# A two-block transformer step in float32 on one core: the order of long and short product rows, four more wide phases, loads and ScalarE copies moved, and the norms' squares added by VectorE in place of Pool

## The reference

```
h = rmsnorm(x, ln1)
hq, hk, hv, hr, ha, hatt, hgate = split(h @ w_in)
o = gated_linear_attention(hq, hk, hv, log_sigmoid(ha @ w_a2 + b_a) / 16)   # 4 heads, chunks of 64
y_gla = (norm(o) * gla_gn * silu(hr)) @ w_o_gla
y_att = dilated_attention(hatt, rel_bias) @ w_o_attn                       # 3 groups, 4 heads
x = x + (sigmoid(g_gla) * y_gla + sigmoid(g_att) * y_att) @ w_out
x = x + relu(rmsnorm(x, ln2) @ w_mlp1) ** 2 @ w_mlp2                        # 4096 wide
x = x + sigmoid(rmsnorm(x, ln3) @ w_pg) * (p @ w_pp)
x = rmsnorm(x, ln_f)
for i in (0, 1):                                                            # second block
    x = x + 0.5 * (silu(n(x) @ ffn1_w1) * (n(x) @ ffn1_w3)) @ ffn1_w2       # 2816 wide
    x = x + (conv_module(n(x)) if i == 0 else mla(n(x), positions))
    x = x + 0.5 * (silu(n(x) @ ffn2_w1) * (n(x) @ ffn2_w3)) @ ffn2_w2
return rmsnorm(x, final_norm)
```

## Time and profile before

| | us |
|---|---|
| median of 3 runs | 1534.92 (1533.19 to 1535.77) |
| the profiled execution | 1532.38 |
| its span | 1530.6 |
| PE busy | 1497.5 |
| DVE busy | 1140.8 |
| ACT busy | 740.9 |
| Pool busy | 99.1 |

### The profile page before, as it was taken

The page is one execution under the profiler, slowest core; times in us unless marked ns, Lnnn a source line. Parts: engine busy times, 40 slices in busy tenths (PEclk is TensorE's granted clock), DMA queues, the critical chain, the costliest instruction groups (busy, mean ns, idle before and its releaser), DMA issues.

```text
span 1530.6 us, 25551 instructions
## 1 busy us (share of the span) xinstructions
PE 1497.5 (98%) x9946; PEld 1336.3 (87%) x9946; DVE 1140.8 (75%) x1466; ACT 740.9 (48%) x996; POOL 99.1 (6%) x144
## 2 busy tenths in 40 slices
PE   8999999999999999999998999999999999999997
PEld 6879899998888988888986988898888997888887
DVE  6767766788866678788876877678776687887754
ACT  5535445534434375554544545345544444455443
POOL 1000000002000121000221100010000010100000
PEclk9999999999999999999999999999999999999999
DMA  7636665456655556656632666567665654466553
GB/s 218 186 96 179 182 177 151 141 184 186 191 191 182 163 176 189 191 155 187 211 117 71 183 191 190 155 193 207 191 185 162 200 135 145 125 180 190 162 170 110
DMA packets 268921, 260.15 MB, mean 170 GB/s; under 512 B 15703, under 2 KB 267173, under 8 KB 268827
## 3 DMA queue, kind: packets, MB, share of 16 engines
q1 hardware_dynamic: 267120, 256.41, 56.3%
q0 software_dynamic: 1072, 1.98, 0.5%
q10 hardware_dynamic: 634, 0.44, 0.1%
HBM read 257.73 MB, written 1.07 MB: 169 GB/s over the span
## 4 chain that ended last, share of the span: by engine, by line
PE 60%; DVE 3%; ACT 1%; issue 1%; POOL 0%; ACTq 0%; DVEq 0%
PE ps L598 28%; PE ps L601 14%; PE ps L605 13%; PE misc L807 2%; PE misc L758 1%; DVE rstd L1239 0%; DVE wsplit L1197 0%; PE misc L639 0%; DVE parts L1215 0%; PE misc L635 0%; DVE plain L1267 0%; PE ps L782 0%; PE misc L761 0%; ACT sq L977 0%; DVE x L1376 0%
## 5 line engine op out<-in xcount | busy, mean ns | idle before, releaser
L1197 DVE TENSOR_TENSOR wsplit<-raw,wsplit 128x1024 fp32r<-128x1024 f32 (+2 forms) x532 | 592.1, 1142 | 106.2 <-ACT wsplit L937 94.8
L937 ACT CAST wsplit<-raw 128x1024 fp32r<-128x1024 f32 (+2 forms) x532 | 494.9, 969 | 179.9 <-DMA raw<-in_ffn_w_dram 89.2
L598 PE MATMUL ps<-xa,wsplit 128*128 128x512 f32 x1504 | 528.2, 397 | 0.0
L601 PE MATMUL ps<-xa,wsplit 128*128 128x256 f32 x1504 | 419.9, 279 | 0.0
L598 PEld LDWEIGHTS ps<-xa,wsplit 128*128 128x128 f32 x1504 | 282.5, 188 | 68.9 <-DVE val L1255 1.4
L598 PE MATMUL ps<-parts,wsplit 128*128 128x512 f32 x924 | 325.3, 397 | 0.2 <-DVEq L1250 0.2
L601 PEld LDWEIGHTS ps<-xa,wsplit 128*128 128x128 f32 x1504 | 283.5, 188 | 0.1
L601 PE MATMUL ps<-parts,wsplit 128*128 128x256 f32 x924 | 259.6, 281 | 0.0
L605 PE MATMUL ps<-parts,wsplit 128*128 128x256 f32 x1740 | 215.2, 286 | 9.7 <-DVE parts L1234 5.5
L605 PEld LDWEIGHTS ps<-parts,wsplit 128*128 128x128 f32 x1740 | 212.1, 194 | 11.1 <-issue 5.9
L965 ACT COPY lohalf<-ps 128x512 f32<-128x512 f32 x140 | 82.0, 586 | 277.0 <-PE ps L601 277.0
(11 more groups left out here) (254 smaller groups left out, 1119.0 us busy)
## 6 DMA issues: line engine op xcount, KB each, us to landing
raw<-in_ffn_w_dram SPq DMA_DIRECT2D x176, 512.0 KB, 3.8
raw<-in_w_in_dram SPq DMA_DIRECT2D x76, 512.0 KB, 3.7
raw<-in_ffn_w_dram SPq DMA_DIRECT2D x96, 384.0 KB, 3.2
raw<-in_w_mlp_dram SPq DMA_DIRECT2D x64, 512.0 KB, 3.7
raw<-in_conv_w_pw_dram SPq DMA_DIRECT2D x24, 512.0 KB, 4.2
raw<-in_ffn_w_dram SPq DMA_DIRECT2D x32, 256.0 KB, 3.1
raw<-in_w_o_gla_dram SPq DMA_DIRECT2D x8, 512.0 KB, 3.4
raw<-in_w_out_dram SPq DMA_DIRECT2D x8, 512.0 KB, 3.4
```

Source lines behind the costliest of these rows:

```text
L598: mm(o, still, both.rearrange("p h t -> p (h t)"), start=st, stop=False, skip_group_check=True)
L601: last = mm(o[:, T:2 * T], still, moves, start=False, stop=en, skip_group_check=True)
L937: nc.scalar.copy(wsplit[:, slot, 0:kn, 0, 0:p.width], raw[:, slot, 0:kn, 1, 0:p.width]).then_inc(hi_done, 1)
L1197: TT(wsplit[:, slot, 0:kn, 1, 0:p.width], raw[:, slot, 0:kn, 1, 0:p.width], wsplit[:, slot, 0:kn, 0, 0:p.width].bitcast(F32), ALU.subtract ...
```

## The change

It does seven things.

1. In wide groups that aren't the first of their phase, PE takes all long rows of a block and then all short ones in even blocks, and all short ones and then all long ones in odd blocks. With layout F the long rows of an even block wait for the high parts only.
2. hr, w_out, pw2 and w_o join the wide phases.
3. DVE adds the squares (`add_squares`), two chunks side by side, in the groups that make x; Pool keeps only the sum of the norm "conv".
4. ACT issues one load (ln1) at the start; the other eleven loads of gains and the six of the setup go behind the norm step of ha. PE turns the gains and computes the relative bias after the second group of gla_q. The first split of x takes two steps.
5. ACT copies the turned probabilities after the first cast of the group instead of after the second.
6. p is loaded by Pool before the convolution's taps, into other memory, turned by PE after mlp2's first group, copied by DVE there.
7. The norm step of ckv moves behind the evacuation of uq_rope's second group.

```diff
-WIDE = (["gla_q", "gla_k", "gla_v", "mlp1", "mlp2"] + [f"att_{w}{g}" for w in "qkv" for g in range(3)]
+WIDE = (["gla_q", "gla_k", "gla_v", "hr", "w_out", "mlp1", "mlp2", "pw2", "w_o"] + [f"att_{w}{g}" for w in "qkv" for g in range(3)]
...
+                    F = p.layout == "F"
...
+                    def high(kk, c, end):
+                        mov, w, wh, _, mh, _ = operands(kk, c)
+                        still, both = (wh, mov) if F else (mh, w)
+                        return mm(ps[:, bank, c, :], still, both.rearrange("p h t -> p (h t)"),
+                                  start=p.k0[j] + kk == 0, stop=end, skip_group_check=True)
+
+                    def low(kk, c, end):
+                        _, _, wh, wl, mh, ml = operands(kk, c)
+                        still, moves = (wl, mh) if F else (ml, wh)
+                        return mm(ps[:, bank, c, T:2 * T], still, moves, start=False, stop=end, skip_group_check=True)
+
+                    places = [(kk, c) for kk in range(kn) for c in range(p.width // P)]
+                    ends = j == len(p.kns) - 1
+                    if p.halves(g) and not first and j % 2 == 0:
+                        if F:
+                            pe.wait_ge(hi_done, lin(s + 1, RING if i is not None else 0, i))
+                        else:
+                            pe.wait_ge(lo_done, lin(s + 1, RING if i is not None else 0, i))
+                        for kk, c in places:
+                            high(kk, c, False)
+                        if F:
+                            pe.wait_ge(lo_done, lin(s + 1, RING if i is not None else 0, i))
+                        for kk, c in places:
+                            last = low(kk, c, ends and kk == kn - 1)
+                    elif p.halves(g) and not first:
+                        pe.wait_ge(lo_done, lin(s + 1, RING if i is not None else 0, i))
+                        for kk, c in places:
+                            low(kk, c, False)
+                        for kk, c in places:
+                            last = high(kk, c, ends and kk == kn - 1)
+                    else:
+                        pe.wait_ge(lo_done, lin(s + 1, RING if i is not None else 0, i))
+                        for kk, c in places:
+                            k = p.k0[j] + kk
+                            if first and c == 0:
+                                pe.wait_ge(ready, p.ready + k + 1)
+                                high(kk, c, False)
+                                last = low(kk, c, en)
+                                continue
...
-                        if p.name == "ha":
-                            pe.wait_ge(s_rows, 16 * (len(GAINS) - 1))
-                            transpose_to(ps[:, 0, 1, 0:GAIN_N], gain_rows, GAIN_N).then_inc(s_pe, 1)
-                        elif g == 0 and p.name in norm_at:
+                        if g == 0 and p.name in norm_at and p.name != "ha":
...
-                        if p.name == "gla_q" and g == 0:
-                            relative_bias()
+                        if p.name == "gla_q" and g == 1:
+                            pe.wait_ge(s_rows, 16 * (len(GAINS) - 1))
+                            transpose_to(gains_turned, gain_rows, GAIN_N).then_inc(s_pe, 1)
+                            relative_bias()
...
-                        if p.name == "w_pg0":
+                        if p.name == "mlp2" and g == 0:
...
-                                                        plain[:, 40 + t, k * P:(k + 1) * P])
+                                                        unit(64 + t)[:, k * P:(k + 1) * P])
```

ACT, at the start and in the loop over the phases:

```diff
-                act.dma_start(gain_rows[at:at + n, :], v.rearrange("(c p) -> c p", p=P)
-                              ).then_inc(s_ln1 if at == 0 else s_rows, 16)
-                at += n
+            act.dma_start(gain_rows[0:NC, :], a["ln1"].rearrange("a (c p) -> (a c) p", p=P)).then_inc(s_ln1, 16)
...
-                if c == 3:
-                    act.dma_start(wa2[0:GLA_RANK, :], a["w_a2"][0]).then_inc(s_setup, 16)
-                    act.dma_start(wa2[GLA_RANK:GLA_RANK + 1, :], a["b_a"]).then_inc(s_setup, 16)
...
+            def small_inputs():
+
+                at = 0
+                for name, n in GAINS:
+                    v = a[name]
+                    v = v if len(v.shape) == 1 else v.rearrange("a n -> (a n)")
+                    if at:
+                        act.dma_start(gain_rows[at:at + n, :], v.rearrange("(c p) -> c p", p=P)).then_inc(s_rows, 16)
+                    at += n
+                act.dma_start(wa2[0:GLA_RANK, :], a["w_a2"][0]).then_inc(s_setup, 16)
+                act.dma_start(wa2[GLA_RANK:GLA_RANK + 1, :], a["b_a"]).then_inc(s_setup, 16)
...
+                act.dma_start(posi, a["positions_2"][0].partition_broadcast(P)).then_inc(s_setup, 16)
...
+                            if j == 0 and ((p.name == "gates" and g % 2 == 0 and g) or p.name == "y_gla0"):
+                                attend(f"att{g // 2 - 1 if g else 3}", ATT_G, "pT")
                         if g == 0 and p.name in norm_at:
                             norm_step(norm_at[p.name])
+                            if p.name == "ha":
+                                small_inputs()
...
-                        if (p.name == "gates" and g % 2 == 0 and g) or p.name == "y_gla0":
-                            attend(f"att{g // 2 - 1 if g else 3}", ATT_G, "pT")
```

DVE, where the sums of squares are called, the function, and the other moved steps:

```diff
+                    if g:
+                        add_squares("cq" if g < 2 else "ckv", 2 if g < 2 else 1)
...
+                if kind == "resid" and g >= 2:
+                    add_squares(pair_of[p.name], g)
                 if kind == "resid":
                     xs = x[:, 2 * g:2 * g + 2, :]
...
+                    if g == 3:
+                        add_squares(pair_of[p.name], 4)
...
+                    if c >= 2:
+                        add_squares("ln_f", c)
...
+                if c == 3:
+                    add_squares("ln_f", 4)
...
+            def add_squares(name, c):
+
+                q, n = pairs[name]
+                if c == n:
+                    v.wait_ge(squared, q + n)
+                if c == 2 or c == n == 1:
+                    v.wait_ge(norm_sum, norms[name])
+                    v.wait_ge(squared, q + min(n, 2))
+                if c == n == 1:
+                    TT(acc[:, 0, :], sq[:, q % 2, 0, :], sq[:, q % 2, 1, :], ALU.add).then_inc(summed, 1)
+                elif c == 2 and n == 2:
+                    step(TT(acc[:, :, :], sq[:, q % 2, :, :], sq[:, (q + 1) % 2, :, :], ALU.add))
+                    TT(acc[:, 0, :], acc[:, 0, :], acc[:, 1, :], ALU.add).then_inc(summed, 2)
+                elif c == 2:
+                    TT(acc[:, :, :], sq[:, q % 2, :, :], sq[:, (q + 1) % 2, :, :], ALU.add).then_inc(summed, 2)
+                elif c > 2:
+                    v.wait_ge(squared, q + c)
+                    v.wait_ge(summed, q + c - 1)
+                    added = TT(acc[:, :, :], acc[:, :, :], sq[:, (q + c - 1) % 2, :, :], ALU.add)
+                    if c < n:
+                        added.then_inc(summed, 1)
+                    else:
+                        step(added)
+                        TT(acc[:, 0, :], acc[:, 0, :], acc[:, 1, :], ALU.add).then_inc(summed, 1)
...
-                split_stored(xa[:, 2 * c:2 * c + 2, :, :], x[:, 2 * c:2 * c + 2, :], 2 * c, 2)
+                after_split()
+                split_gained(xa[:, 2 * c:2 * c + 2, :, :], x[:, 2 * c:2 * c + 2, :], 2 * c, 2)
...
+                        if p.name == "ffn1_up0" and g in (1, 18):
+                            for c in (2,) if g == 1 else (3, 4):
+                                add_squares("ffn1_up0", c)
...
                         if p.name == "w_pg0":
-                            pe_did(v, "pT")
-                            done("ple_free", vec.tensor_copy(units(42, 2), misc[:, 0, :].rearrange(
-                                "p (k t) -> p k t", k=2)))
-                            split(parts[:, 16:18, :, :], units(42, 2), 2)
+                            split(parts[:, 16:18, :, :], units(66, 2), 2)
...
+                        if p.name == "mlp2" and g == 0:
+                            pe_did(v, "pT")
+                            done("ple_in", vec.tensor_copy(units(66, 2), misc[:, 0, :].rearrange(
+                                "p (k t) -> p k t", k=2)))
                         if p.name == "uq_rope" and g == 1:
+                            norm_step("ckv", rstd2)
                             rope_keys()
...
-                        if p.name == "gla_q" and g == 0:
+                        if p.name == "gla_q" and g == 1:
+                            pe_did(v, "gainT")
+                            done("gain", vec.tensor_copy(gain[:, NC:GAIN_N], gains_turned[:, NC:GAIN_N]))
                             relative_bias()
...
                 if p.name == "mla_kr":
                     norm_step("cq")
-                    norm_step("ckv", rstd2)
```

(9 more changed lines are left out.)

## The result

The changed kernel takes 1522.47 us (median of 4 runs, 1521.99 to 1523.4) against 1534.72 us before (4 runs): 12.2 us less, a ratio of 0.9922 with a 95% interval of 0.991 to 0.9934. The forecast was 1519 us, 14.1 us less by its sum. The profiled execution took 1522.38 us with a span of 1520.7, so 10.0 us less than the one of before, 1532.38.

What follows compares the result with a forecast made beforehand. It took TensorE, busy 98% of the span, to bound the kernel. Its terms summed to -14.1 us from the profiled 1532.4 us, giving 1518.3; between that and 1520.8 it said 1519 us, range 1492 to 1530.

Steps and rivals of the forecast that it cites:

- (b): Wide groups' rows: a long row behind a long row loses its 13.3 ns, 31 us, giving 1488 us; chance 0.2.
- (c): Wide groups: the order does nothing (1524 us) or puts all rows at the slower level (1534 us); chance 0.24.
- the term of 5.6 us: Wide groups after the first: 2208 pairs at 346.7 ns instead of 349.2 ns, 5.6 us faster.
- rival (d): Each turn from long to short rows stops PE; over 45 ns each eats the gain, 60 ns gives 1537; chance 0.06.
- lost cover: Behind new wide phases: if the next phase's first group no longer hides DVE's lag, some 0.5 us lost a transition.
- the wait on Pool: Before the norm of w_pp: PE's 1.20 us stall on Pool's add shrinks, 0.4 us gained (0 to 1.2).
- at each of the transitions: DVE's adds of squares: half a us lost at each phase transition, the worst case of +5 us.
- The bound of +5: Slow end of the range for DVE's adds of squares, which were taken as +0.5 us in all (-1 to +5).
- 6.6 us for the stalls: Gain from removed stalls, said to remain with the wide phases' 2.4 us if the row order does nothing.

Runs made afterwards that it cites:

- e3: The changed kernel with hr, w_out, pw2 and w_o narrow again; 1525.05 us.
- e6: The changed kernel with all squares added by Pool, as before the change; 1520.48 us.
- e2: The changed kernel with DVE's adds of chunks 3 and 4 for the norm in ffn1_up0 done after group 1, not in group 18; 1519.44 us.
- e5: The changed kernel with the first split of x in three dependent steps again, the loads left moved; 1524.01 us.
- e7: The changed kernel with ACT's copies of the turned probabilities behind both casts again; 1524.73 us.
- e9: The changed kernel with chunks 3 and 4 added after group 1, p split behind w_pg0's evacuation, ln_f's squares added behind x's update; 1517.62 us.
- e10: The changed kernel with e9's three moves of DVE's work, and long and short rows in turn in mlp1, ffn1_up0, ffn2_up0 and ffn1_up1; 1517.73 us.
- e1: The changed kernel with long and short rows taking turns again in every wide group; 1525.52 us.
- e4: The changed kernel with runs of two long and two short rows in all blocks; 1524.04 us.
- e8: The changed kernel with the long rows first in every block; 1525.98 us.

## Why the prediction was nearly right

**Part 1** had the row right and the sum wrong. A long row behind long rows takes 226.7 ns, so rivals (b), 213.3 ns, and (c) fall. The Trainium skill ("TensorE: Matmul & The Clock Gate", section "Back-to-back issue gap") gives 216 ns for 512 columns as the gap of an isolated row, and about 131 for rows in a stream with their weight loads, which the prediction left out; the rows here show 226.7 where they are shortest, longer than both. What the term of 5.6 us left out is the 20 ns that each run of long rows costs in its first five. I count 156 periods (116 groups of two blocks, 8 in mlp2, 32 in the *_down), 3.1 us, more than the gap between -5.6 and -3.2. That leaves 0.7 us on the other side (3.2 + 3.1 - 5.6), which isn't traced; it is as if the pairs of before had cost 0.3 ns more than the mean of the earlier trace rows says. In kind it is rival (d), a price for a turn, at 20 ns a period in place of the over 90 (two turns at 45) that would have made the change slower.

**Part 2** held: -2.4 forecast, -2.0 read, 2.2 in e3. The cover that the new DVE work needs was there, but only with part 3 beside it: with Pool adding (e6) the three phases behind w_out, pw2 and w_o lose 0.5 us each, just what the prediction gave for lost cover.

**Part 3** is the step that missed most. It summed to +0.1 with the wait on Pool and measured +3.7. Its first half held: behind the first group of ffn1_up0 PE's wait on Pool's add is gone, and 0.8 us with it, where 0.4 was forecast. The second half isn't in the prediction: it laid the cost "at each of the transitions", and overlooked that for this one norm the adds of chunks 3 and 4 stand at group 18, with PE's sum right behind that group's rows. They cost PE 2.32 us of waiting and 1.5 us of lower clock (e2: -3.79 for moving them), and the adds in w_pp2 and w_pp3 cost 0.4. The clock's share isn't fixed: in e5 and e7 the same wait had full rows behind it, and their stage was 1.7 and 1.6 us shorter. The bound of +5 covers the number, but for a cost spread over the transitions, not for this one.

**Part 4** read -3.0 for -1.7, and that is luck for the most part. The first copy did come 0.96 us sooner, but PE's first sum, which waits for ACT's squares, and the block behind it did not (10.60 against 10.45 us). At equal pace of the rows the part gave some 0.5 us (e2 and e5 against before). The other 2.5 us are rows at half pace that the profile of before had and that of after had not.

**Parts 5 and 7** were right in mechanism and too small: -2.6 for -1.9, -2.5 for -1.9, 1.3 us together. In part 5 the waits in the table sum to 1.9, but PE's stages gained 2.6 (e7: 2.63 back). In part 7 the evacuation no longer waits for the second reciprocal, as forecast, and PE's 2.32 us wait is gone; this is read from the two profiles alone.

**Part 6**: -0.7 forecast, -0.4 read. The chain to the bank for w_pp1 did get 0.7 us shorter, as forecast, by DVE's copy, and PE, earlier by the load of p, waits longer there, which the forecast had said too. It had left out that PE's turn of p costs 0.4 us in mlp2, where no wait hides it. And it had not seen that the split of p stood in the same chain, in front of w_pg0's evacuation: moving it behind (e9) gave 1.3 us more.

So 1519 was near 1522.5 by luck as much as by the working. 6.7 us were missed (2.4 in the order, 3.6 in part 3, 0.4 in part 2, 0.3 in part 6), and 2.6 us more in parts 4, 5 and 7 stood against them, half of that the pace at the start; and the medians lie 2.2 us further apart than the two profiles do. A slip in the working changed nothing: rival (c) speaks of 6.6 us for the stalls, where the terms of the sum make 6.1.

## What to carry to other kernels

When work moves to another engine's queue, look for each single place where it lands and who waits right behind it: here one place of nine cost 4.1 us, more than the others gave (1.5 behind w_out, pw2 and w_o, 0.8 behind the first group of ffn1_up0), and moving two adds won 3.8 of it back. Reckon that a stall of PE can cost more than its length: the rows behind the wait of 5.5 us and the two of 2.3 us in ffn1_up0 and before w_pp1 ran at the lower clock in 21 of 28 cases here, for 1.1 to 2.7 us. Before you put a gain down to a change, count the rows at half pace in both profiles. And read the price of a row from a run's own first rows too, not from its steady state alone.

## What the runs showed of the hardware

- **Behind a long wait the clock is lower.** In all twelve profiles the one wait of 5.5 us behind the convolution is followed by 9 to 21 rows at half pace, 1.4 to 2.7 us on top of the wait. In e10 (windows with the columns as above):

```profile
823.00:826.50 3.50, 3.50 (x12) 2.92 (x12) 3.29 (x6) 2.90 (x4) 0.00 (x0) 0.50 0.00 0
830.00:838.00 8.00, 8.00 (x50) 7.18 (x49) 7.45 (x13) 4.17 (x6) 0.00 (x0) 1.00 0.67 194
```

  A pair takes 640 ns in the first (1.2 GHz) and 348 in the second (2.4 GHz). Behind shorter waits it comes or not: the 2.3 us at group 18 had such rows in after, e1, e3, e4 and e8 (7 to 12 rows, 1.4 to 1.9 us) and none in e5 and e7; the 2.3 us before w_pp1 had them in e2, e5, e6 and e7 (12 to 17 rows, 1.1 to 1.7 us) and none in the others. In each of the seven profiles with both waits the rows came behind exactly one of the two. Those before w_pp1 cost 0.2 us at most once ffn1_up0 began, since PE then waited less for DVE in w_pp2 and w_pp3. And behind the 2.32 us of before at 1253.88 24 rows took 3.14 us, at full pace. What decides isn't shown.
- **The early rows.** In the first block of ha rows took 228 ns each in before and 134 in after (from its first row to the sum behind it), and the windows view gives a granted clock of 1.00 for both stretches. There the rows, not the clock column, show the pace.
- **Two levels of strict turns.** 346.7 and 353.3 ns a pair, seen in before, e1 and e10, change inside a stage. At the upper level the pairs take 349, 350 and 361 ns in turn, at the lower all 346 or 347. In ffn1_up0 the change stood behind the two rows of a norm's sum each time, at 565.7 (before), 558.6 (e1) and 658.9 us (e10), but such a sum changed nothing in ffn1_up0 of e10 at 556.6. What sets them stays open.
